# Two query tiles per step in the second attention layer of a two-block network on Trainium2

## The reference, cut to what matters

```
q, k, v, gate = jnp.split(hn @ w_in, 4, axis=-1)
q = rms_norm(q, q_gain) * HEAD_DIM ** -0.5
k = rms_norm(k, k_gain)
logits = q . k + bias            # only keys in a window of 16 columns, else -1e30
p = softmax(logits)
y = (p . v) * silu(gate)
x = x + y @ w_out
```

## Time and profile before

| what | us |
|---|---|
| three runs | 1601.22, 1609.79, 1611.50 |
| median of them | 1609.79 |
| the profiled execution, first to last instruction (its span) | 1602.5 |
| of it: second attention layer, loop over 32 steps and output projection | about 688 to 976 |

### The profile page before, as it was taken

The page is one execution under the profiler, slowest core; times in us unless marked ns, Lnnn a source line. Parts: engine busy times, 40 slices in busy tenths (PEclk is TensorE's granted clock), DMA queues, the critical chain, the costliest instruction groups (busy, mean ns, idle before and its releaser), DMA issues. The chain is left out here.

```text
span 1602.5 us, 29989 instructions
## 1 busy us (share of the span) xinstructions
PE 1536.9 (96%) x11712; PEld 1236.3 (77%) x11712; DVE 807.8 (50%) x1933; ACT 772.9 (48%) x1558; POOL 777.1 (48%) x474
## 2 busy tenths in 40 slices
PE   7999999999999999999999999999987999999997
PEld 5888787878888787767777776677776886778886
DVE  5145455464545457434445324298437754274545
ACT  4654637364554644455666633356754432352322
POOL 3734436262534443366555544326747651475551
PEclk9999999999999999999999999999979999999998
DMA  6323132232413131355444215132000000323331
GB/s 153 105 83 109 53 97 81 82 97 66 121 40 109 53 96 53 79 153 155 139 140 124 66 54 159 40 73 66 15 29 3 4 17 29 105 80 97 95 98 53
DMA packets 239125, 131.00 MB, mean 82 GB/s; under 512 B 28646, under 2 KB 233518, under 8 KB 238968
## 3 DMA queue, kind: packets, MB, share of 16 engines
q1 hardware_dynamic: 231448, 114.09, 25.6%
q10 hardware_dynamic: 7536, 14.98, 3.1%
HBM read 126.62 MB, written 2.43 MB: 81 GB/s over the span
## 5 line engine op out<-in xcount | busy, mean ns | idle before, releaser
L1612 POOL TENSOR_TENSOR w_low<-a_w_raw,w_high 128x1024 fp32r<-128x1024 f32 x70 | 173.4, 2478 | 56.3 <-ACT w_high L1499 56.3
L321 PE MATMUL a_proj<-h_low,w_high 128*128 128x512 f32 x488 | 196.3, 402 | 1.2 <-POOL h_low L1630 1.2
L323 PE MATMUL a_proj<-h_high,w_high 128*128 128x512 f32 x488 | 192.0, 393 | 0.0
L322 PE MATMUL a_proj<-h_high,w_low 128*128 128x512 f32 x488 | 191.1, 392 | 0.0
L1625 POOL TENSOR_TENSOR a_sq_low<-a_sq,a_sq_high 128x512 fp32r<-128x512 f32 x48 | 63.0, 1312 | 249.9 <-ACT a_sq_high L1523 249.9
L907 POOL TENSOR_TENSOR w_low<-b_w_raw,w_high 128x1024 fp32r<-128x1024 f32 x40 | 100.4, 2512 | 97.1 <-ACT w_high L741 97.1
L321 PE MATMUL b_proj<-h_low,w_high 128*128 128x512 f32 x288 | 116.6, 405 | 1.4 <-POOL h_low L946 0.8
L323 PE MATMUL b_proj<-h_high,w_high 128*128 128x512 f32 x288 | 113.6, 394 | 0.0
L322 PE MATMUL b_proj<-h_high,w_low 128*128 128x512 f32 x288 | 113.5, 394 | 0.0
L321 PEld LDWEIGHTS a_proj<-h_low,w_high 128*128 128x128 f32 x488 | 91.7, 188 | 23.8 <-issue 1.4
L323 PEld LDWEIGHTS a_proj<-h_high,w_high 128*128 128x128 f32 x488 | 91.7, 188 | 20.7
(11 more groups left out here) (554 smaller groups left out, 4187.0 us busy)
## 6 DMA issues: line engine op xcount, KB each, us to landing
a_w_raw<-in_a_w_in_dram SPq DMA_DIRECT2D x78, 512.0 KB, 3.7
b_w_raw<-in_b_w_in_dram SPq DMA_DIRECT2D x30, 512.0 KB, 4.1
b_ada_w<-in_ada_w_dram ACTq DMA_DIRECT2D x24, 512.0 KB, 3.7
f_wt<-in_w_in_dram SPq DMA_DIRECT2D x18, 512.0 KB, 3.6
sparse_w_raw<-in_w_in_dram SPq DMA_DIRECT2D x17, 512.0 KB, 3.6
a_bias<-scr_a SPq DMA_DIRECT2D x32, 128.0 KB
a_w_raw<-in_a_w_out_dram SPq DMA_DIRECT2D x8, 512.0 KB, 4.3
b_w_raw<-in_b_w_out_dram SPq DMA_DIRECT2D x8, 512.0 KB, 4.2
```

What stands on the lines that cost most here:

```text
L321: nc.tensor.matmul(out, lh, rl, start=first, stop=False)
L322: nc.tensor.matmul(out, ll, rh, start=False, stop=False)
L323: return nc.tensor.matmul(out, lh, rh, start=False, stop=last)
L1612: nc.gpsimd.tensor_tensor(low(slot_of(b)), raw[:, n % RAW, :, :], high(slot_of(b)), ALU.subtract).then_inc(s_wl, 1)
```

## The change

It touches only the second attention layer. The loop goes over two row tiles per round (t and t+1, t even), and the buffers for logits, probabilities and turned probabilities are doubled so that each tile of a round has its own.

- `step_tile(t)`: even tiles use the two score banks (`b_scores`), odd tiles the two banks called `b_turned`. Scores of a tile go into its banks, and the turned probabilities of the tile two before it are written back into the same banks afterwards.
- The products with v go into columns 128 to 383 of the bank of `mod` (`b_mod`), two tiles beside each other, and `keep_y` gates 256 tokens at once.
- Per round PE makes: scores of t and t+1; the turn of v at a pair's first round; the first projection; turns of tiles t-2 and t-1; the second projection; `apply_v` of t-2 and t-1.
- ACT and DVE are put in a new order to match; the pieces of `ada_w` are loaded two at the end of each round, and added one in the middle and one late in the round.

The core of the diff:

```diff
+        o_tile = lambda t: ps_mod[:, (2 - t % 2) * P:(3 - t % 2) * P]
+        step_tile = lambda t: ps_pt if t % 2 else ps_s
...
             def turn(t, h):
...
-                if t:
-                    pe.wait_ge(s_y, t)
...
+                if t + 2 < STEPS:
+                    pe.wait_ge(s_l2, 2 * (t + 2) + h + 1)
                 for c in range(n):
-                    bank, c0 = L.turn_at(h, c)
-                    mm = nc.tensor.transpose(ps_pt[:, bank, c0:c0 + P], probs[:, h, c * P:(c + 1) * P], T.ident)
+                    mm = nc.tensor.transpose(step_tile(t)[:, h, c * P:(c + 1) * P], probs[:, t % 2, h, c * P:(c + 1) * P], T.ident)
...
+            def b_steps():                                   # PE
+                for t in range(0, STEPS + 2, 2):
                     p, r = divmod(t, ROWS)
                     if t < STEPS:
                         scores(t)
+                        scores(t + 1)
                     if p and r == 0 and t < STEPS:
                         project(p, UNITS - 1)
                     if p < PAIRS - 1:
                         project(p + 1, r)
                     elif t < STEPS:
+                        pe.wait_ge(s_y, t // 2 - 1)
+                        for n in range(6 * r, 6 * r + 12):
                             modulate(n)
+                        for k in range(2 if r else 0):
+                            early_out(k)
                     if t:
+                        for back in (2, 1):
+                            turn(t - back, 0)
+                            turn(t - back, 1)
+                    if p < PAIRS - 1:
+                        project(p + 1, r + 1)
+                    elif t < STEPS and r:
+                        for k in range(2, KT - 2):
+                            early_out(k)
+                    if t:
+                        apply_v(t - 2)
                         apply_v(t - 1)
...
+            def b_steps():                                   # ACT
+                for t in range(0, STEPS + 2, 2):
                     p, r = divmod(t, ROWS)
                     if t < STEPS:
+                        for s in (t, t + 1):
+                            exps(s, 0)
+                            exps(s, 1)
+                    if p < PAIRS - 1 and r:
+                        inv_norm(p + 1, r - 1)
+                    if t < STEPS:
+                        for s in (t, t + 1):
+                            act_normal(s, 0)
+                            act_normal(s, 1)
                     if p < PAIRS - 1:
                         after_projection(p + 1, r)
                     elif t < STEPS:
+                        for k in range(2 * r, 2 * r + 2):
+                            y_high(k)
+                    if t:
+                        keep_pt(t - 2, 0)
+                        keep_pt(t - 1, 0)
+                    if p < PAIRS - 1:
+                        if r == 0:
+                            inv_norm(p + 1, 0)
+                        after_projection(p + 1, r + 1)
...
+                    for n in (t - 1, t):
+                        if n > 0 and ADA_SLOTS + n - 1 < MODS:
+                            act.wait_ge(s_as, n)
+                            load_ada(ADA_SLOTS + n - 1)
...
             def keep_y(t):
...
+                nc.vector.tensor_tensor(Y[:, p, r * P:(r + 2) * P][:, ::-1], ps_mod[:, P:3 * P],
+                                        gate[:, p % 2, r * P:(r + 2) * P][:, ::-1], ALU.mult).then_inc(s_y, 1)
...
             def b_steps():                                   # DVE
+                for t in range(0, STEPS + 2, 2):
                     p, r = divmod(t, ROWS)
                     if t < STEPS:
+                        for s in (t, t + 1):
+                            soft_peak(s, 0)
+                            soft_peak(s, 1)
                     if p and r == 0 and t < STEPS:
                         take(p, UNITS - 1)
+                    if t < STEPS:
+                        for s in (t, t + 1):
+                            invert(s, 0)
+                            invert(s, 1)
                     if p < PAIRS - 1 and r:
                         take(p + 1, r - 1)
                     if t < MODS:
                         add_ada(t)
                     if t:
+                        keep_pt(t - 2, 1)
+                        keep_pt(t - 1, 1)
+                    if p < PAIRS - 1:
+                        take(p + 1, r)
+                    if t < MODS:
+                        add_ada(t + 1)
+                    if p < PAIRS - 1 and r:
+                        take(p + 1, r + 1)
+                    if t:
+                        keep_y(t - 2)
```

220 lines of the change are left out of this document (54 added, 166 removed).

## The result

The changed kernel takes 1673.2 us (median of 6 runs, 1666.1 to 1680.7) where the kernel before, on the same chip, takes 1605.8 (6 runs, 1601.2 to 1611.5): 1.0428 of it, 95% interval 1.0404 to 1.0452. That is 67 us slower. 44 us were forecast; the 1673 us lie inside the range of 1628 to 1675, two microseconds from its end. The direction was right, and the size was a third too small.

What follows compares the result with a forecast made beforehand. The prediction took PE's own instructions to bound the loop. Its terms, -8 + 26 + 11 + 14 + 1 = +44 us, against the three-run median of 1609.8 us gave 1654 us, with a range of 1628 to 1675.

Steps and rivals of the forecast that it cites:

- fewer changes of shape: PE changes its array shape at seven places fewer per pair, 0.17 us each, over seven pairs: 8 us less.
- six waits at the turn of v: At a pair's end PE waits 4.4 us for a late ada piece and the taking of v, six times: +26 us.
- five waits ahead of v's projection: In a pair's first round PE waits 2.2 us for the take of k behind a late piece, five times: +11 us.
- clock: PE's granted clock falls to 0.50 behind all six long gaps and half the five short ones: +14 us, bounds 7 and 25.
- last pair: PE waits some 2.5 us for ACT's copies, against about 2 us saved at the layer's end: +1 us, between -1 and +4.
- the last paragraph: Signs to check, among them that the seventh pair, without ada pieces, takes 30.1 us; at 31 or more the gain is wrong.
- Rival 2: The odd ada pieces are issued early enough and not late, so only the gain is left: -7, 1603 us; chance 0.09.
- Rival 1: The waits in the loop come but smaller, and the clock falls less: +28, 1638 us, down to 1626; chance 0.24.
- rival 3: Waits on the banks replace PE's shape changes and the ada pieces happen to be in time: about 1610 us; chance 0.05.
- The upper bound of 25 us: Most that the clock could cost: slow stretches behind all eleven gaps in the loop, a few of them twice.
- the reading of the prediction: The Trainium skill's rule on DMA waits between matmuls: all eleven gaps would pay, 19 us in place of 14, 1659 us.

Runs made afterwards that it cites:

- experiment 2: The changed kernel with ada pieces issued one round earlier and ACT's four normalizations moved behind the square and high part of the round's first projection: 1604.6 us, ratio 0.9996.
- Experiment 7: The kernel of experiment 2 with PE doing v, scores, v, scores in place of v, v, scores, scores: 1609.1 us, ratio 1.0030 to the kernel before.
- Experiment 1: The changed kernel with one line different, issuing each ada piece one round earlier: 1612.8 us, ratio 1.0054 to the kernel before.
- experiment 3: The kernel before, one tile per step, with only the six ada pieces of a pair's last step issued late: 1654.0 us, ratio 1.0310.
- experiment 4: The changed kernel with idle products on PE in its gaps, 40 ahead of turns of v and 20 ahead of v's projection: 1666.4 us, ratio 1.0382.
- experiment 5: The kernel of experiment 3 with 44 idle products on PE in each of its six waits: 1640.9 us, ratio 1.0226 to the kernel before.
- experiment 6: The changed kernel, ada pieces left late, with only the four normalizations moved behind the round's first projection's square and high part: 1660.2 us, ratio 1.0344.
- experiment 8: Four kernels, each that of experiment 2 with edits to the last pair's early products, modulation products or high parts of y: 1607.5, 1603.5, 1604.6 and 1597.0 us.
- the fourth kernel of experiment 8: The third kernel there, with more of the last pair's high parts of y made ahead of ACT's four normalizations: 1597.0 us, ratio 0.9959 to the kernel before.

## Why the prediction came out as it did

The time came out inside the range, and part of that is luck. The range was built on the median of three runs, 1609.8 us, and six runs have 1605.8. As a difference its upper end was +65 us, and +67 were measured. The two kinds of wait that were forecast are right in place, number and size; the clock, a wait that was missed and the last pair are each too small in the forecast.

Forecast and finding for each term, over the windows above. The finding compares the changed kernel with experiment 2, in which the late pieces and the wait for `b_sq_low` are mended: 286.0 - 216.2 = 69.9 us for the seven pairs.

| term | forecast | found |
|---|---|---|
| fewer changes of shape | -8 | -6.2 (216.2 against 222.3) |
| six waits at the turn of v | +26 | +26.1 |
| five waits ahead of v's projection | +11 | +11.7 |
| waits of the sums for `b_sq_low` | none | +4.5 (6.7, of which 2.2 stay) |
| clock | +14 | +27.6 (the rest of the 69.9) |
| last pair | +1 | +5.9 |
| sum | +44 | +69.6 (span: +67.2) |

*Fewer changes of shape: right.* A pair without waits takes 30.15 us, the 30.1 of the forecast. Experiment 7 shows the 0.175 us per change by adding some. The 6.2 us are less than 8 because the stretch from the first to the second turn of v, which holds the start of the layer, did not get shorter (35.3 against 34.8 us; it varies from 33.2 to 35.6 between the kernels here). The seventh pair of the changed kernel took 33.0 us, not 30.1, so by the letter of the last paragraph the gain would have been called wrong: it held a wait of 1.0 us for `b_sq_low` and 3.4 us at 0.50 that began in the gap ahead of it. The test was badly chosen, since it took the pair for undisturbed.

*The waits at the turn of v and ahead of v's projection: right, place, number and size.* DVE stood at the odd pieces 11 times, PE 6 and 5 times. Rival 2 (pieces not late) is excluded by these waits. Experiment 1, which makes the pieces early, does not reach that rival's 7 us under the kernel before, since the waits for `b_sq_low` and the last pair stay. Rival 1 (smaller waits) and rival 3 fall with the table.

*The clock: mechanism right, size half.* The step that failed is "I take six gaps of 4.4 us as followed by one such stretch each, and half of the five gaps of 2.2 us". In or behind all eleven gaps a stretch at 0.50 began, six of them 6.8 us long and not 3.4, and at the first pair's start another of 6.8: 64.9 us in all, in which PE was busy for 53.9, so that it lost 26.9 (before 1.7, in experiment 2 3.4). So 23.5 of the 27.6 us are these stretches; some 4 us stay without a name. The upper bound of 25 us, "all eleven, a few twice", was what happened: the stretches cost 25.2 us more than before. By the reading of the prediction all eleven gaps would pay, and that was nearer than my choice. The Trainium skill (TensorE: Matmul & The Clock Gate, section Loop structure matters more than you think), from which I had it, shows a long DMA wait ahead of each matmul, behind which PE runs cold; its example is of a longer wait than any here. Why a stretch is 3.4 or 6.8 us long is open. It isn't that a second gap follows: in experiment 3, with one gap per pair, the six were 6.8 or 10.2 us long, and the gap of 2.7 us at the layer's start had 3.4 us behind it in eight of the thirteen profiles, 6.8 in four and nothing in one. Experiments 4 and 5 show by filled gaps that the gaps cause the fall; in experiment 4 the clock gives 19.6 us back, and 9.5 of them go into longer waits.

*The normalization's wait: missed.* I wrote that "the doubled buffers, the gating of 256 tokens and the doubled reciprocal waits lie on engines with 12 to 15 us of room per pair and cost nothing by themselves". Room of 12 us in ACT does not help an instruction that is queued behind one that waits. The diff has the wait (`s_Tb if h else s_Ta, t - 1`) and the order has the turns behind the first projection; I did not put the two together. It is 4.5 us of waits in the table, but experiment 6 shows 13.5 us for it (with the two intervals, 8 to 19), and with it out no stretch at 0.50 follows the second gap of a pair. Whether that is the shorter gap (1.8 us) or what PE did ahead of it was not separated.

*The last pair: wait right, sum too small.* The wait of 2.5 us for the copies came as forecast (2.5 us at L625). I took +1 us with "a possible slow stretch of the clock"; there were 10.2 us at 0.50. In experiments 1, 2, 4, 6 and 7 it was even 17.1 us, and the last pair some 9 us longer than before. The step that failed is that the two serial microseconds which go at the layer's end were set against it, while the clock got next to nothing. Behind its turn of v the last pair's first round had almost nothing but thin products for PE, and the early products stood a round later; moved up alone they had to wait for `h_low`, and only with the high parts ahead of ACT's waits did the loss go (experiment 8).

## What to carry to other kernels

When a schedule is coarsened (two tiles per step), list for every in-order queue what now stands behind an instruction that waits, and for whom: here a DMA issued in the same round as its use, and a normalization that waits for a read of its buffer, each held up work that had nothing to do with them. Where TensorE never idles, expect more than the wait itself from each new gap: in this layer 35 us of waits, 5.0 to 7.0 us each, brought 13 us of clock, and 42 us, most of them 2.0 to 4.6 each, brought 28. Two kernels are no rule, but a third to two thirds of the waits is a fairer first guess than nothing. Ask also of a small wait whether it changes a gap behind which the clock then falls. A gain that doesn't show in the total may be there: cut the trace at fixed events, compare the windows, and look for the one that grew.

## What the runs showed of the hardware

- In or behind the gap ahead of v's projection the clock fell to 0.50 when the gap was 2.6 us (three pairs of the changed kernel) and 2.0 us (two pairs), and it stayed at 1.00 when it was 1.8 us (five pairs of experiment 6). The length of a gap does not decide alone: in experiment 5 the clock fell for 6.8 us where PE waited 1.3 us behind 44 idle products, and in experiment 4 it did not fall where PE waited 1.4 us behind 40.
- The same gap of 2.7 us at the start of the layer had a stretch of 3.4 us at 0.50 behind it in eight of the thirteen profiles, one of 6.8 in four, and none in one (the fourth kernel of experiment 8).
- A long stretch at 0.50 (17.1 us) came without an idle gap of more than 2 us, in the last pair of experiment 2, where PE did matmuls of 128x1 and 128x128 and waited 2.0 us. In the kernel before, with as many thin products in smaller groups and early products between most of them, the clock stayed at 1.00 there. With the early products moved up it was 3.4 to 6.8 us (experiment 8). Which of the products and the waits lets it fall was not separated.
- The late ada pieces at a pair's end took 3.8 to 4.6 us from issue to landing in the changed kernel, and 6.6 and 5.5 us at two of six places in experiment 4, issued as soon after the projection (0.1 and 0.4 us). In experiment 6 they took 4.1 to 5.7 us. What made them land later was not tried.
